# Spreading a second half-batch over 236 gathered rows, with a lag of three rows for the lanes and three stages of row buffers

## The reference, cut to what matters

```python
def peer_ffn(x, w_query, sub_keys, expert_u, expert_v):
    ...
        q = (xb @ w_query).reshape(PEER_TOKEN_BLOCK, PEER_HEADS, 2, PEER_HALF)
        sc = jnp.einsum('thpd,hpkd->thpk', q, sub_keys).astype(jnp.float32)
        s_top, i_top = lax.top_k(sc, PEER_TOPK)
    ...
        g = jax.nn.softmax(best, axis=-1)
        u = jnp.take(expert_u, eidx, axis=0)
        h = jax.nn.gelu(jnp.einsum('thkd,td->thk', u, xb))
        vv = jnp.take(expert_v, eidx, axis=0)
        return jnp.einsum('thk,thkd->td', (g * h.astype(jnp.float32)).astype(xb.dtype), vv)
```

## Time and profile before

| | us |
|---|---|
| median of 3 runs | 3584.49 (3583.04 to 3586.76) |
| the profiled execution, its own time | 3589.76 |
| its span, from the first to the last instruction | 3587.6 |
| its mean granted PE clock (share of full speed) | 0.874 |
| first gather of a row starts | 2101.7 |
| last row's multiply on DVE starts | 3573.5 |

### The profile page before, as it was taken

One profiled execution on the slowest core, in us unless ns is written; L12 is line 12 of the kernel. 1 busy time (PEld: TensorE's weight loads), 2 busy tenths in 40 slices (PEclk: granted clock), 3 DMA queues, 4 the chain that ended last, 5 costly groups with the idle time before them and its releaser, 6 DMA issues.

```text
span 3587.6 us, 43456 instructions
## 1 busy us (share of the span) xinstructions
PE 2821.2 (79%) x17054; PEld 1419.8 (40%) x17054; DVE 1611.5 (45%) x3373; ACT 991.9 (28%) x2369; POOL 693.1 (19%) x602
## 2 busy tenths in 40 slices
PE   7678888888599999999998977877687556555555
PEld 6457666338333333333336764433352111111111
DVE  3744854645310101001102246655556777677674
ACT  2123123331000000000002334564344344333432
POOL 0411411000000000000000013323334444444442
PEclk9889988689799999999999888987797787777777
DMA  2220211321899999999994268977899999999997
GB/s 110 72 69 24 90 69 37 135 82 37 348 420 420 420 420 420 420 419 420 420 420 155 97 273 346 401 292 281 315 410 396 420 420 420 420 420 420 420 419 325
DMA packets 155996, 1068.83 MB, mean 298 GB/s; under 512 B 17296, under 2 KB 19088, under 8 KB 30352
## 3 DMA queue, kind: packets, MB, share of 16 engines
q0 software_dynamic: 75408, 543.20, 37.3%
q1 hardware_dynamic: 80384, 522.87, 36.1%
HBM read 1052.63 MB, written 13.37 MB: 297 GB/s over the span
## 4 chain that ended last, share of the span: by engine, by line
PE 55%; DMA 24%; DVE 13%; ACT 6%; issue 2%; POOL 0%; SPq 0%; DVEq 0%; ACTq 0%; POOLq 0%
PE ps L92 52%; DMA gb<-in_peer_uv,eidx 22%; DVE gb L146 3%; PE ps L97 2%; DMA ring<-in_wt 1%; ACT dots L168 1%; ACT L168 1%; ACT diag L168 1%; DVE inv_x L115 1%; DVE wa_lo L115 1%; DVE wa_hi L130 1%; DVE expert_act L115 1%; DVE rw_t L134 1%; POOL gb L86 0%; DVE rw_t L115 0%
## 5 line engine op out<-in xcount | busy, mean ns | idle before, releaser
L92 PE MATMUL ps<-gb,diag 64*64 64x512 f32 x4096 | 688.9, 791 | 489.1 <-ACT diag L168 483.5
L146 DVE CUSTOM_DVE_ANT_0 gb<-gb,xn 128x1024 f32<-128x1024 f32 x512 | 625.7, 1223 | 328.5 <-DMA gb<-in_peer_uv,eidx 319.0
L86 POOL DMA_INDIRECT gb<-in_peer_uv,eidx x512 | 557.4, 1089 | 1079.2 <-PE ps L92 818.5
L92 PEld LDWEIGHTS ps<-gb,diag 64*64 64x64 f32 x4096 | 147.1, 160 | 954.3 <-ACT diag L168 872.6
L92 PE MATMUL ps<-ga,xt 128*64 128x512 f32 x1120 | 331.4, 601 | 2.5 <-DVE xt L120 2.5
L115 DVE TENSOR_TENSOR expert_act<-expert_act,ps 128x512 f32<-128x512 f32 x32 | 22.0, 687 | 541.7 <-PE ps L92 541.2
L168 ACT ACTIVATE dots<-dots 128x1 f32<-128x1 f32 (+1 forms) x346 | 70.3, 203 | 665.2 <-DVE dots L146 658.0
L115 DVE TENSOR_TENSOR x<-x,ps 128x512 f32<-128x512 f32 (+1 forms) x96 | 61.4, 643 | 418.2 <-PE ps L92 417.8
L168 ACT ACTIVATE diag<-cons,dots 128x128 f32<-128x128 f32 x512 | 205.5, 401 | 38.7 <-ACT dots L168 0.4
L92 PE MATMUL ps<-h_hi,wa_hi 128*128 128x512 f32 x368 | 163.5, 444 | 43.2 <-DVE wa_lo L115 39.3
L92 PEld LDWEIGHTS ps<-ga,xt 128*64 128x64 f32 x1120 | 118.9, 137 | 187.6 <-issue 180.5
(11 more groups left out here) (317 smaller groups left out, 3849.2 us busy)
## 6 DMA issues: line engine op xcount, KB each, us to landing
ring<-in_wt SPq DMA_DIRECT2D x77, 1024.0 KB
ga<-in_eg SPq DMA_DIRECT2D x70, 1024.0 KB, 26.4
ga<-in_eu SPq DMA_DIRECT2D x70, 1024.0 KB, 27.1
ga<-in_ed SPq DMA_DIRECT2D x68, 1024.0 KB, 27.7
gr<-in_eu SPq DMA_DIRECT2D x37, 1024.0 KB, 26.8
gr<-in_ed SPq DMA_DIRECT2D x34, 1024.0 KB, 27.7
ring<-in_eg SPq DMA_DIRECT2D x29, 1024.0 KB, 26.4
gr<-in_eg SPq DMA_DIRECT2D x29, 1024.0 KB, 27.2
```

Of the source, the lines that this page charges most:

```text
L86: self.e.indirect_dma_start(out, None, table, bass.IndirectOffsetOnAxis(ap=idx, axis=0)).then_inc(s, 16)
L92: i = self.e.matmul(out, l, r, start=st, stop=sp, skip_group_check=True)
L146: self.done(self.e.tensor_tensor_reduce(out=o, in0=a, in1=b, scale=scale, scalar=start, op0=o0, op1=o1, accum_out=acc), name)
```

## The change

It alters three things.

1. The order. The 51 steps of pass 1 stand after rows 4, 7, 11, 14, 18, ... (`pass_rows`, 18 rows to 5 steps), the last after row 184, and the lanes' part of a step stands three rows behind PE's part. The 8 query tiles of the second pass stand after rows 190, 196, ..., 232 on PE, and ACT's copy of each four rows behind it.
2. The row buffers. Three of the seven later ones (`MIDDLE`: the keys, the values and the attention result) are used from row 172, after the last tile of the output projection; the other four (`LATE`: the 3 ring slots and `f_t`) from row 236 (`GROW`), after the last query tile. A table (`ROW_SLOTS`) gives row n an unused buffer where there is one, and otherwise the one whose row is oldest: 6, then 9, then 13 buffers in turn.
3. ACT finds the PSUM bank of a query tile or a score by its name, as others now come between.

Rows go one by one up to 235 instead of 179.

```diff
--- before.py
+++ after.py
@@ -2073,17 +2073,24 @@
     low, tot, inv = (small[:, 64 + 32 * n:96 + 32 * n] for n in range(3))
     io16 = cons[:, C_IOTA:C_IOTA + 16].rearrange("p (a b) -> p a b", a=1)
     EARLY = [M(f"gb{i}", 29744 + 2048 * i, 2048) for i in range(5)] + [M("gb5", 2048, 2048)]
-    LATE = [T(f"gb{6 + i}", O_RING + 2048 * i, 2048) for i in range(3)]
-    LATE += [M(f"gb{9 + i}", o, 2048) for i, o in enumerate((10240, 12288, 16384, 18432))]
-    STEPS, GROW = 27, 180
+    MIDDLE = [M(f"gb{6 + i}", o, 2048) for i, o in enumerate((10240, 12288, 16384))]
+    LATE = [T(f"gb{9 + i}", O_RING + 2048 * i, 2048) for i in range(3)] + [M("gb12", 18432, 2048)]
+    STEPS, GROW = 27, 236
     VB = [6, 7]
 
-    def row_slot(n):
-
-        if n < GROW:
-            return n % 6, (n - 6 if n >= 6 else None)
-        m = (n - GROW) % 13
-        return (6 + m, n - 13 if n >= GROW + 13 else None) if m < 7 else (m - 7, n - 13)
+    ROW_BUFFERS = [(t, 0, None) for t in EARLY]
+    ROW_BUFFERS += [(t, 172, ("used", TILES + P0 - 1)) for t in MIDDLE]
+    ROW_BUFFERS += [(t, GROW, ("used", 2 * TILES - 1)) for t in LATE]
+
+    def row_slots():
+
+        held, slots = [None] * len(ROW_BUFFERS), []
+        for n in range(512):
+            s = min((held[s] is not None, held[s] if held[s] is not None else s, s) for s, (_, first, _) in enumerate(ROW_BUFFERS) if n >= first)[2]
+            slots.append((s, ROW_BUFFERS[s][2] if held[s] is None else ("sum", held[s])))
+            held[s] = n
+        return slots
+    ROW_SLOTS = row_slots()
 
     def row_group(n):
 
@@ -2099,6 +2106,7 @@
         yield ("s", 0, 0)
         yield ("t", 0, 0)
         done, p, owed = 0, 2, []
+        pass_rows = [4 + 18 * k // 5 for k in range(51)]
         n = 0
         while n < 512:
             group = row_group(n)
@@ -2122,14 +2130,14 @@
             yield ("w", group)
             if group[-1] % 128 == 127:
                 yield ("out", group[-1] // 128)
-            if 4 <= n < 134 and n % 5 in (0, 2):
+            if n - 3 in pass_rows:
+                yield ("n",)
+            if n in pass_rows:
                 yield ("m",)
-            if 4 <= n < 134 and n % 5 in (1, 3):
-                yield ("n",)
-            if 134 <= n < 174 and n % 5 == 4:
-                yield ("p", 1, (n - 134) // 5)
-            if 134 <= n < 174 and n % 5 == 1:
-                yield ("q", 1, (n - 136) // 5)
+            if 0 <= n - 190 < 48 and (n - 190) % 6 == 0:
+                yield ("p", 1, (n - 190) // 6)
+            if 0 <= n - 194 < 48 and (n - 194) % 6 == 0:
+                yield ("q", 1, (n - 194) // 6)
             n = group[-1] + 1
 
     def sp_peer(sp):
@@ -2193,7 +2201,7 @@
                           XN[i][64 * r:64 * r + 64, 512:1024], name=("total", i) if r else None)
 
     def buf_of(n):
-        return (EARLY + LATE)[row_slot(n)[0]]
+        return ROW_BUFFERS[ROW_SLOTS[n][0]][0]
 
     def ac_peer(ac):
         ac.signals("act_mix2")
@@ -2202,21 +2210,21 @@
             pass
         ac.signals("act_peer")
         turn, wide, few, _ = after_pass(turn, wide)
-        second, banks = ac_pass(ac, 1, turn, wide), []
+        second, banks = ac_pass(ac, 1, turn, wide), {}
         for ev in peer_order():
             if ev[0] == "n":
                 next(second, None)
             elif ev[0] in ("p", "s"):
-                banks.append(few.next())
+                banks[ev] = few.next()
             elif ev[0] == "q":
                 p, m = ev[1:]
-                b, use, _ = banks.pop(0)
+                b, use, _ = banks[("p", p, m)]
                 ac.wait_ge(("used", TILES * p + P0 + m))
                 ac.act(QT[p][:, 2 * m:2 * m + 2, :], pair(PS[b]), ACT.Copy, name=use)
                 ac.mark(("query", p, m))
             elif ev[0] == "t":
                 i, h = ev[1:]
-                b, use, _ = banks.pop(0)
+                b, use, _ = banks[("s", i, h)]
                 ac.wait_ge(("score_ps", i, h))
                 if 8 * i + h >= 2:
                     ac.wait_ge(("sc_free", i, h - 2) if h >= 2 else ("sc_free", i - 1, h + 6))
@@ -2346,12 +2354,10 @@
         po_mix2(po)
         for n in range(512):
             i, k = n // 128, n % 128
-            s, before = row_slot(n)
+            s, freed = ROW_SLOTS[n]
             po.wait_ge(("eidx", i, k // 16))
-            if before is not None:
-                po.wait_ge(("sum", before))
-            elif n >= GROW:
-                po.wait_ge(("used", 2 * TILES - 1))
+            if freed is not None:
+                po.wait_ge(freed)
             po.gather(buf_of(n), I["peer_uv"], eidx[i % 2][:, k:k + 1], f"gb{s}", ("row", n))
```

## The result

| | before | after |
|---|---|---|
| median of 4 runs of each, us | 3584.47 (3583.04 to 3586.76) | **3530.74** (3524.34 to 3535.42) |
| profiled execution, its own time | 3589.76 | 3530.28 |
| its span; mean granted PE clock | 3587.6; 0.874 | 3528.3; 0.881 |
| first gather to last row's multiply | 1471.8 | 1421.8 |

The ratio is 0.9848, with a 95% interval of 0.9831 to 0.9865: faster by 53.7 us, where 71 were forecast. Of the 59.5 us between the two profiled executions only 50.0 lie in the stretch of the 512 rows. Most of the rest lies ahead of it: the first gather started at 2092.9 instead of 2101.7, in a stage that the change doesn't touch.

The account below looks back on a forecast made before the run. DMA at 420 GB/s was taken as the bound, empty for 115.8 us, mostly beside the second pass. Leaving 9 + 20 + 7 + 7.7 = 43.7 gains 72: 3517.7 profiled, 3513 us median, range 3486 to 3555.

Parts of the forecast that it names:

- the gate: At row 236, gather 236 and all behind it wait for the last query tile: DMA empty about 7 us.
- rows 50 to 181: Second pass from row 50 on: empty DMA time falls from 90.5 to 20 us, ends 5 and 50.
- the end of block 0 at row 127: Together with two norms after the output projection, where ACT and DVE wait for each other: 6 us left empty.
- 8 for the second: Attention's second half, where PE is tightest: 8 us of DMA time left empty.
- The lag of three rows: In second pass steps, PE gets three rows, 7.5 us, before the lanes: 80.4 us of DVE waiting go.
- the spacing step: 3.6 rows per step instead of 2.5; rows 70 to 159: DMA longest at 239 us, PE 231.5, or 97%.
- PE becomes the bound: Rival: PE needs a tenth more than its busy time beside the second pass; gain 44, 3541 us, chance 19%.
- The new buffers: Rows 172 to 179, going from six to nine buffers: cost nothing.
- the holds turn round: Rival: PE waits for the lanes, each of 51 steps still leaves 2.0 us empty; slower, 3597 us, chance 5%.
- DMA was full in truth: Rival: rows 6 to 255 already at a memory limit of some 360 GB/s; no change, 3584 us, chance 2%.
- Table switches at twice their load: Rival: attention steps hold ACT 6.6 us, 0.7 above the slack, 13 us in 19 steps; 3526 us, chance 4%.
- all of it goes: Rival: only 4 + 5 + 3 + 7.7 us stay empty; gain 96, 3488 us, chance 14%.

Follow-up runs that it names:

- after_again: The changed kernel run once more with no edit: 3531.85 us, ratio 0.9861.
- share_load: Changed kernel, with the choice's exp waiting for the attention's next one to share its table load, 5 of 139 loads fewer: 3536.64 us, ratio 0.987.
- spacing_only: Changed kernel's spacing, query tiles and buffers, but with the lanes' part one row behind PE's as before: 3534.75 us, ratio 0.9869.
- pe_warm: Changed kernel plus two matmuls that add zero before each of the rows 96 to 139: 3530.86 us, ratio 0.985.
- rows_tanh: Changed kernel with the rows' gelu replaced by tanh (another result), so 83 table loads go: 3519.12 us, ratio 0.9814.
- no_middle: Changed kernel, but the three MIDDLE buffers come into use only from row 236, leaving six until then: 3534.92 us, ratio 0.9859.
- weighted: Changed kernel with LATE buffers from row 242, block added three multiplies later, and steps spaced by their cost: 3524.03 us, ratio 0.9825.

## Why the prediction was right or wrong

**The mechanism: right, with its two halves taken for one.** The stages beside the second pass run nearer to 420 GB/s, either remedy alone does most of it, and the total is inside the range. Three of the four terms came out near: rows 6 to 29 with 9.0 us (forecast 9, ends 4 and 17), the rest with 8.0 in rows 30 to 49 and 240 to 511 (7.7), the gate with 9.1 (7, ends 2 and 12). The base matters too. The prediction took the median 5.3 us below the profiled execution of before; the one of after is 0.5 below its median. Some of the closeness of the profiled executions (forecast 3517.7, measured 3530.28) is luck: in the stretch 22 us of the gain of 72 are missing, and 9.5 came outside it, where the change does nothing.

**The term that was mis-sized: "For rows 50 to 181 (90.5 us empty before) I take 20 left".** It was 1.5 + 5.7 + 17.7 + 15.3 = 40.2 us, inside its ends of 5 and 50, and this is nearly all of the difference between 44 and 66. Two of its parts were mis-sized.

- *"6 for the end of block 0 at row 127 and the two norms after the output projection."* The norms cost nothing (rows 140 to 181: 0), the block's end with the last attention steps 15.3, after 16.2 before. The prediction named the place but did not write down its chain: last `diag`, last two rows on PE with an attention step between, ACT's copy, PE's transposes, DVE's addition, with the next block's first multiply behind it. The addition waited 11.7 us with a slack of 5.9, and moving it behind three multiplies gave back 7 us in each of the two traces that have it alone or with the gate (6 against after_again's 14.5).
- *"8 for the second"* half of the attention. It was 17.7 (15.4 in after_again), of which 7 to 10 go with the table loads. The prediction counted two loads and an exp per lanes' step, some 4 us, and compared that one hold with 5.9 of slack. The choice's exp adds a pair of loads in some steps, so four stand close together there, 5.1 us in all. That two holds in a row share one slack would explain the miss, but it is argued: share_load, made to test it, removed one such meeting of two and gained nothing. The trace shows a hold that the prediction's two loads per step leave out (ACT, and PE's wait for it):

```profile
2457.31 1.28 ACT L168 ACT_TABLE_LOAD   x1
...
2458.60 0.20 ACT L168 ACTIVATE small<-small 128x2 f32<-128x2 f32 x1
...
2459.40 1.28 ACT L168 ACT_TABLE_LOAD   x1
...
2461.71 1.98 PE L92 MATMUL ps<-gb,diag 64*64 64x512 f32 x8 [5.30 <-ACT diag L168]
```

The square root of the gate's norm stands there between an exp and the next gelu. With the exp's first load, at 2455.23, these are three loads, and 6.5 us pass from one row's `diag` to the next; PE's wait of 5.30 is the longest of the stage. Nor are such gaps rare: in rows 100 to 126 nine times 4.9 to 6.5 us passed between two `diag`, with tanh six times 4.6 to 5.8. What makes up the other 8 us stays open.

**"The lag of three rows ... The 80.4 us of DVE waiting go."** They did go, but for 3.6 at `prob` and 11.7 at `x`, and those last are the block's end (the prediction left out 23.8 at `a_t`, of which 13.7 stayed). But the prediction let this stand for the gain. spacing_only keeps 79.4 us of waiting and has the same empty DMA time. The argument needed one more question: whether a wait is longer than the slack once steps come every 3.6 rows.

**The PE part of the spacing step: right in the verdict, wrong in the mix.** The prediction gave rows 70 to 159 the 25 steps that had stood beside rows 70 to 130. Those were the last 25 of the 51, with 12 of the attention's 19; in the changed kernel rows 70 to 159 hold steps 20 to 44, with all 19. The window of these 90 rows, 2312.3 to 2597.3:

```profile
2312.30:2597.30 285.00, 219.16 (x1152) 101.52 (x1156) 185.44 (x468) 171.66 (x395) 104.06 (x90) 0.83 0.91 363
```

PE was busy 219 us where 231.5 were forecast, DVE 185 where 189.5 were, but ACT 172 where 151 were. The bytes took 246 us of full rate (239 forecast), so PE needed 89% of that and not 97%. The granted clock did not change much: 0.79, 0.84 and 0.66 before in rows 70 to 99, 100 to 126 and 127 to 139, and 0.84, 0.82 and 0.64 after. The rival that PE becomes the bound (3541) is not borne out: in pe_warm PE is busy 12 us more in rows 100 to 126, at a higher clock, and no more DMA time is lost, and rows_tanh gains in the same rows with PE's work as it was.

**The new buffers: "Cost nothing", "held by nine buffers": right.** no_middle shows that six would not have held the tiles: they lost 8.8 us. So the prediction's "a hold on one engine every few rows is free", read from 1.5 us lost in 90, was too kind to six buffers. The kernel before lost 6.5 in rows 140 to 181, where its eight tiles stood, 5.0 of them in the last twelve rows.

**The other rivals.** That the holds turn round (3597): PE waited 118.3 us for ACT's `diag`, little more than the 113.5 before, and next to nothing for `prob`; rows 6 to 181 left 51 us of DMA time empty, 1.0 per step and not 2.0. That DMA was full in truth (3584): rows 140 to 229 ran 249 us at 420 with the second pass beside them. The Trainium skill (DMA: Bandwidth & Descriptors, Specifications) works its limit of about 358 GB/s out as a stack's bandwidth shared by two cores. This trace is of one core, and its 420 lies above that figure. Table switches at twice their load (3526) came near in time and not in cause, since the idle time before a load is 0.07 us. That all of it goes (3488): no experiment came near; the best has 49 us left.

**Two of the signs were bad.** "POOL's wait for PE no longer the largest by far" did not come (333.1 before, 334.4 after), nor could it: while DMA is full POOL has nothing to do but wait for the next buffer, so its wait tells nothing of the slack. And rows 50 to 181 "at over 390 GB/s" failed as an average, 378, while four of the six stages were at 394 to 420 and two, rows 100 to 139, at 337 and 286: a sign for so long a stretch doesn't tell where it fails.

**The best version found** is both, which has the changed kernel's order with the gate at row 242 and the block's addition three multiplies later: 3519.39. Its four executions and the four of weighted, which contains it, took 3512.87 to 3524.99; the changed kernel's eight took 3524.34 to 3536.01.

**What stays open**: how the table loads come to cost 14 to 17 us, the 8 us that rows 100 to 126 lose without them, 9 in rows 6 to 29, and every difference below some 6 us.

## What to carry to other kernels

Where one resource should stay full, write down per stage the time it stands empty and change only what that table points at; two remedies for the same slack, such as a longer lag and a wider spacing, don't add, so each wants its own run. Check a new spacing with the steps that will stand in each stretch, not with those that stood there. Write the chain of holds out at the points where all engines meet, such as a block's end, and put the whole of it against the slack. In an in-order queue a buffer that isn't free yet should come into use late rather than as soon as its row number is reached, because everything behind it waits too.

## What the runs showed of the hardware that was not expected

- The stage before the first gather, the same program in all these kernels, ended anywhere from 2092.9 to 2105.1 us. That spread of 12.2 us is wider than most differences between two of the experiments.
- PE slows down for a while after it has waited. A row's 8 matmul records took 1.98 to 1.99 us after waits of 3.70 to 5.30 and 1.09 at best, about the ratio of its two levels, 1.2 and 2.4 GHz. The granted clock was 0.64 in rows 127 to 139, a mixture of both. Work that adds zero brought it to 0.96 there and to 0.95 in rows 100 to 126, yet the kernel's time stayed.
- A long sum of work off the critical path is no price: taking away 83 table loads, 106 us of ACT's time at 1283 ns each, was worth 12.7 us of the kernel's.
